# GQA attention: the second chunk's softmax reciprocal and its last multiplications come six steps later, behind the short chunk's

## The chip, the cores and the metric

One core of a Trainium2 chip runs the whole program. The metric is device time in microseconds (us). Before the change it is 3407.32 us, the median of three runs (3406.72 to 3411.54).

## What is computed

The reference is a block with sliding-window attention and an FFN, then two hybrid layers: one with grouped-query attention (GQA), one with MLA. The change lies in the GQA attention of the first hybrid layer alone:

```python
def gqa_attend(q, k, v):
    s = jnp.einsum('bqhgd,bkhd->bhgqk', q, k).astype(jnp.float32) * (GQA_HEAD_DIM ** -0.5)
    p = jax.nn.softmax(s, axis=-1).astype(v.dtype)
    return jnp.einsum('bhgqk,bkhd->bqhgd', p, v)
# 16 heads of 64; 1024 image queries see 256 + 1024 keys, 256 context queries see the 256 context keys;
# afterwards the output is multiplied by silu(g)
```

## The kernel before

**Chunks and steps.** Each head has three chunks of queries: chunk 0 and chunk 1 with 512 queries and ten tiles of 128 keys, and chunk 2, the short one, with 256 queries and two tiles of keys. One step is one tile of keys of one chunk, so a head has 22 steps: 0 to 9 are chunk 0, 10 to 19 chunk 1, 20 and 21 chunk 2. Heads follow each other without a break. Two heads make one turn of the loop, 44 steps. In this text a step number is that of its own head, and "a boundary" is the stretch in which one head ends while the next one runs its first steps.

**One step.** TensorE computes the transposed scores with two matrix products into one of two PSUM banks (L2371, L2372). ScalarE takes exp into `PF` (L2424) and rounds it into `PH` (L2430). GpSimd subtracts the two to get the low part `PL` (L2473); for steps 7, 9, 13 and 19 VectorE does this instead. TensorE then multiplies high and low parts with the values, three products into the output bank of the chunk (L2386 to L2388), three steps behind the scores. Chunks 0 and 1 have output banks of their own. Chunk 2 uses the bank `BC`, which also carries the transposed row maxima. The value tiles hold ones in their upper half, so the denominator stands in partitions 64 to 127 of the output bank.

**Row maxima.** The next chunk's maxima are prepared beside the steps: TensorE computes a tile of scores into `PMX` (L2341), VectorE reduces it (L2498), and when a chunk's tiles are done TensorE transposes them (L2352) and VectorE writes the row into `Q` (L2506). `PMX` holds one such tile, so TensorE can write the next one only when VectorE has reduced the one before. The plan by steps: tiles of the same head's chunk 1 at steps 0 (taken with the head before), 2 and 4, the short chunk's at 6, rows at 8 and 11, then the next head's chunk 0 at steps 10, 12, 14 and 16, its chunk 1's first at 18, a row at 20. In the last head steps 10 to 20 of this plan fall away.

**The end of a chunk.** ScalarE computes the reciprocal of the denominator with Ln and Exp into `RD` (L2440, L2442, function `rden`), between the exp and the rounding of a step. VectorE multiplies the output by it into `T` (L2517) and then `T` by the gate into `MIX` (L2522, function `final`). `RD` is one buffer, so a reciprocal waits for the multiplication into `T` before it. The counter `norm` counts these multiplications, and TensorE waits for it before it starts a chunk's output bank again.

**The order.** Each engine runs its own list, written out by hand. `lags` says how many steps behind its last step a chunk's end comes: on ScalarE 4, 4 and 5 steps for chunks 0, 1 and 2, on VectorE 8, 5 and 6. Within a step VectorE's list has first the maxima or row, then the low part of the step before where it is VectorE's, then the end of a chunk:

```python
if k and self.dve_lo(k - 1):
    self.low(dve, i, k - 1)
...
self.run(dve, step, lambda i, k: self.ended(final, i, k, self.lags), max(self.lags), ...)
```

So the head before has its chunk 1 reciprocal in step 1 and its end in step 2 of this head, and its chunk 2 reciprocal in step 4 and end in step 5.

SyncE issues the loads of keys, queries, values and the gate; the gate of a pair of heads is loaded once all ends of the pair before are done. After the last head, `MixSplit` splits `MIX` into a high and a low part (ScalarE L1889, VectorE L1893) for the output projection, the first three slices ahead of the last head's ends.

Of the kernel before, what the change touches and what calls it, by code (L numbers as in the profile page):

```python
# [104 lines left out]
def mixed_program(nc, A, out):  # L105

    ctx = ExitStack()
    with ctx:

        def sem(name):  # L110
            return ctx.enter_context(nc.semaphore(name))
# [4 lines left out]
        class Scope:  # L116


            def __init__(self):
                self.stack = ExitStack()  # L120
# [1981 lines left out]

        CR_PV2, CR_SC, CR_B, CR_E, CR_ROW2, CR_R, CR_N, CR_FIN2 = 4, 1, 2, 2, 1, 1, 4, 1

        def head_buffers(name, scope, q, layout, nq, side="left"):

# [8 lines left out]
        class Attention:  # L2117
# [9 lines left out]
            def __init__(self, name, scope, chunks, keys, scale, layout, mix, first, first_maxima):  # L2127
                self.name, self.chunks, self.keys, self.scale, self.mix = name, chunks, keys, scale, mix
                self.mla = layout == "mla"
                self.row = 96 if self.mla else 64  # L2130

                self.K, self.Q, self.V = zip(first, head_buffers(name, scope, 1, layout, chunks[-1][0] + chunks[-1][1]))
                self.G = scope.sb(f"{name}_gate", [P, chunks[-1][0] + chunks[-1][1]])
                self.PF = [scope.sb(f"{name}_pf{b}", [P, C]) for b in range(4)]
                self.PH = [scope.sb(f"{name}_ph{b}", [P, C], R32) for b in range(4)]
                self.PL = [scope.sb(f"{name}_pl{b}", [P, C], R32) for b in range(4)]
                self.M = first_maxima
                self.dim = 96 if self.mla else 64
                self.nq = chunks[-1][0] + chunks[-1][1]
                self.load_inc = 16 * (4 if self.mla else 6)  # L2140

                self.const_n = 32 + 4 + (32 + 2 if self.mla else 0)
                self.v_and_const = [sem(f"{name}_v_and_const{q}") for q in range(2)]
                self.RD = scope.sb(f"{name}_rd", [64, C])
                self.T = scope.sb(f"{name}_t", [P, C])
                self.loaded = [sem(f"{name}_loaded{q}") for q in range(2)]
                self.gate_loaded = sem(f"{name}_gate_loaded")
                (self.max, self.red, self.bcast, self.row_done, self.scores, self.exp, self.hi,
                 self.lo_pool, self.lo_dve, self.pv, self.rden, self.norm, self.fin) = [sem(f"{name}_{x}") for x in (
                     "max", "red", "bcast", "row", "scores", "exp", "hi", "lo_pool", "lo_dve", "pv",  # L2150
                     "rden", "norm", "fin")]
                self.S = [PB[0], PB[1]]
                self.BC = PB[2]
                self.FREE = self.BC if self.mla else PMX[:, 0:C]
                self.O = [PD[0], PD[1], self.BC]

                self.steps = [(q, c, t, x == 0, x == len(keys[c]) - 1) for q in range(2) for c in range(len(chunks))
                              for x, t in enumerate(keys[c])]
                self.SB = len(self.steps)
                self.NC = len(chunks)  # L2160

                if self.mla:
                    plan = [(2 * t, "max", (0, 1), t) for t in range(4)] + [(8, "bcast", (0, 1), 0)]
                    plan += [(10 + 2 * t, "max", (1, 0), t) for t in range(4)] + [(18, "bcast", (1, 0), 0)]
                    self.ahead = [(0, t) for t in range(4)]
                else:
                    plan = [(2 * t - 2, "max", (0, 1), t) for t in range(1, 4)] + [(6, "max", (0, 2), 0)]
                    plan += [(8, "bcast", (0, 1), 0), (11, "bcast", (0, 2), 0)]  # L2170
                    plan += [(10 + 2 * t, "max", (1, 0), t) for t in range(4)]
                    plan += [(18, "max", (1, 1), 0), (20, "bcast", (1, 0), 0)]
                    self.ahead = [(0, t) for t in range(4)] + [(1, 0)]
                self.plan = plan
                tiles = [p[2] for p in plan if p[1] == "max"]
                self.NT = len(tiles)
                self.last_tile = {group: n for n, group in enumerate(tiles)}
                self.fin_all = HEADS * self.NC + CR_FIN2
                self.norm_all = HEADS * self.NC + CR_N

                self.dve_lo = lambda k: k % (self.SB // 2) in ((3, 8, 13, 18) if self.mla else (7, 9, 13, 19))
                self.lags = (self.LAG + 4, self.LAG + 4, 0) if self.mla else (self.LAG + 5, self.LAG + 2, self.LAG + 3)
                self.n_dve = sum(1 for k in range(self.SB) if self.dve_lo(k))
                self.n_pool = self.SB - self.n_dve

# [134 lines left out]
            def pe_begin(self, pe):  # L2320
# [3 lines left out]
                SB, NC = self.SB, self.NC  # L2324
# [20 lines left out]
                def bcast(i, c, g, tile):  # L2345
                    n = self.chunks[c][1]
                    pe.wait_ge(self.red, i * (2 * self.NT) + (tile + CR_R + 1))

                    pe.wait_ge(self.row_done, i * (2 * NC) + (g + CR_ROW2))
                    if NC == 3:  # L2350
                        pe.wait_ge(self.norm, i * (2 * NC) + ((g - 1) // NC * NC + CR_N))
                    pe.matmul(self.BC[0:4, 0:n], self.M[g % 2][:, 0:4], ident[:, :].unsqueeze(1).to_broadcast([P, n // P, P]),  # L2352
                              start=True, stop=True).then_inc(self.bcast, 1)

# [20 lines left out]
                def values(i, k):  # L2375
                    q, c, t, first, last_ = self.steps[k]
                    n = self.chunks[c][1]
                    self.wait_lo(pe, i, k)
                    if first and c == 0:
                        pe.wait_ge(self.v_and_const[q], i * 32 + self.const_n)  # L2380
                    if first:

                        pe.wait_ge(self.norm, i * (2 * NC) + (q * NC + c - NC + CR_N + 1))
                    o = self.O[c][:, 0:n]
                    ph, pl = self.PH[k % 4][:, 0:n], self.PL[k % 4][:, 0:n]
                    pe.matmul(o, self.V[q][0][:, t, :], ph, start=first, stop=False)  # L2386
                    pe.matmul(o, self.V[q][1][:, t, :], ph, start=False, stop=False)  # L2387
                    pe.matmul(o, self.V[q][0][:, t, :], pl, start=False, stop=last_).then_inc(self.pv, 1)  # L2388
# [26 lines left out]
            def act_begin(self, act):  # L2415
                act.sem_inc(self.exp, CR_E)
                SB, NC = self.SB, self.NC
# [14 lines left out]
                def rden(i, k):  # L2432

                    q, c = self.steps[k][:2]
                    n = self.chunks[c][1]
                    x = q * NC + c
                    act.wait_ge(self.pv, i * SB + (k + CR_PV2 + 1))

                    act.wait_ge(self.norm, i * (2 * NC) + (x + CR_N))
                    act.activation(self.RD[:, 0:n], self.O[c][64:128, 0:n], ACT.Ln).then_inc(self.rden, 1)  # L2440
                    act.wait_ge(self.rden, i * (4 * NC) + (2 * x + 1))
                    act.activation(self.RD[:, 0:n], self.RD[:, 0:n], ACT.Exp, scale=-1.0).then_inc(self.rden, 1)  # L2442
# [1 line left out]
                def step(i, k, last, between):  # L2444
                    probs(i, k, between)

                lags, lag = (self.LAG + 1, self.LAG + 1, self.LAG + 2), self.LAG + (1 if self.mla else 2)

                def rest(split):
                    act.preload_act_table_set(LN_EXP)  # L2450
# [34 lines left out]
            def dve_begin(self, dve):  # L2485
                SB, NC, R = self.SB, self.NC, 2 * self.NT
# [23 lines left out]
                def final(i, k):  # L2510
                    q, c = self.steps[k][:2]
                    o, n = self.chunks[c]
                    x = q * NC + c
                    h = slice(64 * q, 64 * q + 64)
                    dve.wait_ge(self.rden, i * (4 * NC) + (2 * x + 2))
                    dve.wait_ge(self.fin, i * (2 * NC) + (x + CR_FIN2))
                    dve.tensor_tensor(self.T[h, 0:n], self.O[c][0:64, 0:n], self.RD[:, 0:n], ALU.mult)\  # L2517
                       .then_inc(self.norm, 1)
                    dve.wait_ge(self.norm, i * (2 * NC) + (x + CR_N + 1))
                    dve.wait_ge(self.gate_loaded, i * 16 + 16)  # L2520
                    m = self.mix[h, bass.ds(i, 1), o:o + n].rearrange("p o n -> p (o n)")
                    dve.tensor_tensor(m, self.T[h, 0:n], self.G[h, o:o + n], ALU.mult).then_inc(self.fin, 1)  # L2522
# [1160 lines left out]
```

## Time and profile before

| | |
|---|---|
| median of three runs | 3407.32 us |
| the profiled execution, its own time | 3410.39 us |
| its span | 3408.6 us |
| granted TensorE clock, mean | 0.993 |
| busy: TensorE, VectorE, ScalarE, GpSimd | 97%, 66%, 51%, 45% |
| GQA attention, from the first scores to the last values | 1770.5 to 2271.6 us |
| one turn of the loop (two heads) | 62.0 us |

The busy share of TensorE is no measure of its speed: a matrix product of 512 columns is shown as 390 ns long, while the next one starts 230 ns after it. So the starts are to be read, not the lengths. A wait of a few tenths hides in such a row.

### The profile page before, as it was taken

The page shows a single profiled execution, that of the slowest core. Times are in us where ns is not written, and L with a number is a line of the kernel's source. Part 1 is how long each engine was busy: PE and PEld are TensorE (multiplying, and loading weights), DVE is VectorE, ACT ScalarE, POOL GpSimd, SP SyncE. Part 2 cuts the span into 40 slices and gives each one's busy share as a digit, 9 for nine tenths or more (in the row PEclk, how much of TensorE's full clock was granted, in tenths as well). Part 3 has the DMA queues.
Part 4 walks back from the last instruction along what each step waited for, and adds up shares of the span by engine and source line. Part 5 has one row for each costly group of instructions (what it writes and reads, how often), then busy time and mean ns, then how long its engine had stood idle before and what let it go on. Part 6 is the DMA issues. An engine that isn't in the chain of part 4 may idle for free.

```text
span 3408.6 us, 48047 instructions
## 1 busy us (share of the span) xinstructions
PE 3292.7 (97%) x15029; PEld 2641.6 (77%) x15029; DVE 2259.8 (66%) x2664; ACT 1728.5 (51%) x2961; POOL 1522.3 (45%) x958
## 2 busy tenths in 40 slices
PE   9999999999999999999999999999998989999999
PEld 7778878778888888778877777778675668888877
DVE  7684878677576675648627777767558886666661
ACT  4343878332010111334328988871465658888880
POOL 2303444644444445520037777777220016666663
PEclk9999999999999999999999999999999999999999
DMA  3134231411212122123354354423255444332312
GB/s 111 50 117 132 56 89 51 154 53 55 91 48 94 49 75 73 39 85 111 121 138 89 81 108 100 88 65 116 102 193 157 130 128 120 69 80 62 80 38 80
DMA packets 196105, 313.57 MB, mean 92 GB/s; under 512 B 100944, under 2 KB 111696, under 8 KB 195984
## 3 DMA queue, kind: packets, MB, share of 16 engines
q1 hardware_dynamic: 195984, 312.01, 31.7%
q8 instruction: 70, 1.15, 0.1%
q14 instruction: 51, 0.42, 0.0%
HBM read 234.02 MB, written 77.92 MB: 92 GB/s over the span
## 4 chain that ended last, share of the span: by engine, by line
PE 64%; POOL 11%; issue 9%; DVE 9%; ACT 4%; DMA 1%; SPq 1%; POOLq 0%; DVEq 0%; ACTq 0%
PE PBX L285 11%; PE PBX L286 10%; PE PBX L287 10%; POOL gqa_pl L2473 9%; PE PMX L285 4%; PE PMX L286 4%; PE PMX L287 4%; PE PD L2386 2%; PE PMX L2341 2%; PE PD L2387 2%; PE PD L2388 2%; PE PBX L2368 2%; PE PBX L2367 2%; PE PBX L2369 2%; PE PD L1114 2%
## 5 line engine op out<-in xcount | busy, mean ns | idle before, releaser
L218 POOL TENSOR_TENSOR w_hi<-w_stage,zero 128x1024 fp32r<-128x1024 f32 (+2 forms) x114 | 222.3, 1950 | 1147.2 <-PE PBX L287 729.9
L2473 POOL TENSOR_TENSOR gqa_pl<-gqa_pf,gqa_ph 128x512 fp32r<-128x512 f32 (+1 forms) x288 | 371.1, 1309 | 141.2 <-ACT gqa_ph L2430 138.9
L2473 POOL TENSOR_TENSOR mla_pl<-mla_pf,mla_ph 128x512 fp32r<-128x512 f32 x256 | 341.4, 1339 | 194.6 <-ACT mla_ph L2430 189.6
L2498 DVE TENSOR_REDUCE mla_m<-PMX 128x1 fp32r<-128x1280 f32 x128 | 190.8, 1491 | 165.7 <-PE PMX L2341 165.6
L220 POOL TENSOR_TENSOR w_lo<-w_stage,w_hi 128x1024 fp32r<-128x1024 f32 (+2 forms) x114 | 289.2, 2537 | 9.0
L2498 DVE TENSOR_REDUCE gqa_m<-PMX 128x1 fp32r<-128x1280 f32 x144 | 201.5, 1399 | 133.1 <-PE PMX L2341 132.4
L2010 ACT ACTIVATE conv_in<-PBX 128x512 f32<-128x512 f32 x66 | 39.5, 599 | 478.8 <-PE PBX L287 474.8
L2424 ACT ACTIVATE mla_pf<-PBX 128x512 f32<-128x512 f32 x320 | 191.0, 597 | 81.8 <-PE PBX L2369 68.1
L2424 ACT ACTIVATE gqa_pf<-PBX 128x512 f32<-128x512 f32 (+1 forms) x352 | 200.0, 568 | 43.1 <-PE PBX L2372 40.4
L2430 ACT ACTIVATE gqa_ph<-gqa_pf 128x512 fp32r<-128x512 f32 (+1 forms) x352 | 215.0, 611 | 12.1
L285 PE MATMUL PBX<-ffn_hi,w_hi 128*128 128x512 f32 x528 | 206.8, 392 | 4.7 <-DVE ffn_lo L788 4.7
L2430 ACT ACTIVATE mla_ph<-mla_pf 128x512 fp32r<-128x512 f32 x320 | 201.9, 631 | 11.4
L287 PE MATMUL PBX<-ffn_hi,w_lo 128*128 128x512 f32 x528 | 205.5, 389 | 0.0
L286 PE MATMUL PBX<-ffn_lo,w_hi 128*128 128x512 f32 x528 | 205.5, 389 | 0.0
L2039 DVE SCALAR_TENSOR_TENSOR conv_out<-conv_in,VEC,conv_out 128x1024 f32<-128x1024 f32 x88 | 188.0, 2136 | 12.8 <-DVE conv_out L2035 0.6
L285 PE MATMUL PBX<-l_hi,w_hi 128*128 128x512 f32 (+1 forms) x400 | 157.8, 395 | 8.6 <-DVE l_lo L788 6.8
L484 DVE SCALAR_TENSOR_TENSOR PMX<-mod_w,cond_s 128x1024 f32<-128x1024 f32 x96 | 158.7, 1653 | 5.7 <-DVE PMX L484 0.8
L2035 DVE TENSOR_SCALAR conv_out<-conv_in,VEC 128x1024 f32<-128x1024 f32 x44 | 72.2, 1641 | 135.5 <-ACT conv_in L2010 134.7
L1723 POOL TENSOR_TENSOR swa_pl<-swa_pf,swa_ph 128x512 fp32r<-128x512 f32 x64 | 81.6, 1275 | 157.1 <-ACT swa_ph L1648 156.8
L287 PE MATMUL PBX<-l_hi,w_lo 128*128 128x512 f32 (+1 forms) x400 | 144.6, 361 | 0.0
L286 PE MATMUL PBX<-l_lo,w_hi 128*128 128x512 f32 (+1 forms) x400 | 144.4, 361 | 0.0
L285 PE MATMUL PBX<-h_hi,w_hi 128*128 128x512 f32 x336 | 139.0, 414 | 4.3 <-DVE h_lo L591 2.3
(534 smaller groups left out, 9882.1 us busy)
## 6 DMA issues: line engine op xcount, KB each, us to landing
mod_w<-in_w_mod SPq DMA_DIRECT2D x48, 512.0 KB, 3.5
w_stage<-in_w_up SPq DMA_DIRECT2D x44, 512.0 KB, 3.4
w_stage<-in_w_go SPq DMA_DIRECT2D x24, 512.0 KB, 3.7
gqa_k<-kh_d SPq DMA_DIRECT2D x32, 320.0 KB, 4.8
gqa_q<-qh_d SPq DMA_DIRECT2D x32, 320.0 KB, 7.0
w_stage<-in_w_down SPq DMA_DIRECT2D x24, 384.0 KB, 3.1
qh_d<-heads_qh SPq DMA_DIRECT2D x32, 256.0 KB, 2.1
ql_d<-heads_ql SPq DMA_DIRECT2D x32, 256.0 KB, 2.3
```

Of the source, the lines that this page charges most:

```text
L218: pool.tensor_tensor(w_hi[s][:, 0:st.cols], w_stage[s][:, 0:st.cols], z, ALU.add).then_inc(w_hi_done, 1)
L220: pool.tensor_tensor(w_lo[s][:, 0:st.cols], w_stage[s][:, 0:st.cols], w_hi[s][:, 0:st.cols].bitcast(F32), ALU.subtract).then_inc(w_split, 1)
L285: pe.matmul(ps, wh, xh, start=first, stop=False)
L286: pe.matmul(ps, wh, xl, start=False, stop=False)
L287: return pe.matmul(ps, wl, xh, start=False, stop=last)
L484: dve.scalar_tensor_tensor(out=PMX[:, C:3 * C], in0=bufs[s], scalar=1.0, in1=conds[j], op0=ALU.mult, op1=ALU.mult, accum_out=MOD[:, bass.d ...
L1723: pool.tensor_tensor(swa_PL[K % 4][:, :, 0:m], swa_PF[K % 2][:, :, 0:m], swa_PH[K % 4][:, :, 0:m].bitcast(F32), ALU.subtract).then_inc(a1[ ...
L2039: dve.scalar_tensor_tensor(out=y, in0=CU[s][:, j:j + S], scalar=w(j), in1=y, op0=ALU.mult, op1=ALU.add).then_inc(conv_step, 1)
L2424: act.activation(self.PF[k % 4][:, 0:n], self.S[k % 2][:, 0:n], ACT.Exp, scale=self.scale)\
L2430: act.activation(self.PH[k % 4][:, 0:n], self.PF[k % 4][:, 0:n], ACT.Copy).then_inc(self.hi, 1)
L2473: eng.tensor_tensor(self.PL[k % 4][:, 0:n], self.PF[k % 4][:, 0:n], self.PH[k % 4][:, 0:n].bitcast(F32), ALU.subtract).then_inc(self.lo_dv ...
L2498: dve.tensor_reduce(self.M[g % 2][:, t:t + n], PMX[:, 0:n * w].rearrange("p (n w) -> p n w", n=n), AX.X, ALU.max, negate=True).then_inc(se ...
```

## The change

On ScalarE chunk 1's reciprocal comes 10 steps behind the chunk's last step in place of 4. On VectorE its end comes 11 steps behind in place of 5. In the next head's count this is step 7 in place of 1, and step 8 in place of 2. The short chunk's stay in steps 4 and 5, so they now come first; `place` gives the new order for the counters, and `CR_N`, the credit of the counter `norm`, goes from 4 to 5, so that the waits mean the same buffers. MLA, which uses the same class, keeps its order.

```diff
-        CR_PV2, CR_SC, CR_B, CR_E, CR_ROW2, CR_R, CR_N, CR_FIN2 = 4, 1, 2, 2, 1, 1, 4, 1
+        CR_PV2, CR_SC, CR_B, CR_E, CR_ROW2, CR_R, CR_N, CR_FIN2 = 4, 1, 2, 2, 1, 1, 5, 1
...
-                self.lags = (self.LAG + 4, self.LAG + 4, 0) if self.mla else (self.LAG + 5, self.LAG + 2, self.LAG + 3)
+                self.place = (0, 1) if self.mla else (0, 2, 1)
+                self.lags = (self.LAG + 4, self.LAG + 4, 0) if self.mla else (self.LAG + 5, self.LAG + 8, self.LAG + 3)
...
                     if NC == 3:
-                        pe.wait_ge(self.norm, i * (2 * NC) + ((g - 1) // NC * NC + CR_N))
+                        pe.wait_ge(self.norm, i * (2 * NC) + ((g - 1) // NC * NC - 1 + CR_N))
...
-                        pe.wait_ge(self.norm, i * (2 * NC) + (q * NC + c - NC + CR_N + 1))
+                        pe.wait_ge(self.norm, i * (2 * NC) + (q * NC + self.place[c] - NC + CR_N + 1))
...
-                    x = q * NC + c
+                    x = q * NC + self.place[c]
                     act.wait_ge(self.pv, i * SB + (k + CR_PV2 + 1))
...
-                lags, lag = (self.LAG + 1, self.LAG + 1, self.LAG + 2), self.LAG + (1 if self.mla else 2)
+                lags = (self.LAG + 1, self.LAG + (1 if self.mla else 7), self.LAG + 2)
+                lag = max(lags[:NC])
...
-                    x = q * NC + c
+                    x = q * NC + self.place[c]
                     h = slice(64 * q, 64 * q + 64)
```

## Rows read from the trace of the kernel before

**Rows 1.** The page, the chain that ended last, by line.

```profile
PE PBX L285 11%; PE PBX L286 10%; PE PBX L287 10%; POOL gqa_pl L2473 9%; PE PMX L285 4%; PE PMX L286 4%; PE PMX L287 4%; PE PD L2386 2%; PE PMX L2341 2%; PE PD L2387 2%; PE PD L2388 2%; PE PBX L2368 2%; PE PBX L2367 2%; PE PBX L2369 2%; PE PD L1114 2%
```

**Rows 2.** Waits within the GQA attention: total us, times, longest.

```profile
PEld PD L2386 <- POOL gqa_pl L2473: 32.2, 81, 0.7
...
PE PMX L2341 <- DVE gqa_m L2498: 1.6, 2, 1.0
```

**Rows 3.** Timeline of TensorE, an odd head's steps 4 to 12: start, length, what.

```profile
1873.01 0.40 PE L2371 MATMUL PBX<-gqa_q,gqa_k 128*128 128x512 f32 x1
...
1873.64 0.50 PE L2386 MATMUL PD<-gqa_ph,gqa_v 128*128 128x512 f32 x1
...
1876.39 0.40 PE L2371 MATMUL PBX<-gqa_q,gqa_k 128*128 128x512 f32 x1
...
1877.54 0.39 PE L2371 MATMUL PBX<-gqa_q,gqa_k 128*128 128x512 f32 x1
...
1884.45 0.73 PE L2341 MATMUL PMX<-gqa_k,gqa_q 128*128 128x512 f32 x3
1885.02 0.40 PE L2371 MATMUL PBX<-gqa_q,gqa_k 128*128 128x512 f32 x1
```

**Rows 4.** Timeline of TensorE, the even head before it: its steps 4 and 12.

```profile
1841.96 0.39 PE L2371 MATMUL PBX<-gqa_q,gqa_k 128*128 128x512 f32 x1
...
1854.05 0.40 PE L2371 MATMUL PBX<-gqa_q,gqa_k 128*128 128x512 f32 x1
```

**Rows 5.** Timeline of ScalarE, the odd head's steps 1 to 12.

```profile
1869.82 0.59 ACT L2424 ACTIVATE gqa_pf<-PBX 128x512 f32<-128x512 f32 x1
...
1871.60 0.61 ACT L2430 ACTIVATE gqa_ph<-gqa_pf 128x512 fp32r<-128x512 f32 x1
...
1872.86 0.63 ACT L2430 ACTIVATE gqa_ph<-gqa_pf 128x512 fp32r<-128x512 f32 x1
...
1874.55 0.58 ACT L2424 ACTIVATE gqa_pf<-PBX 128x512 f32<-128x512 f32 x1
...
1875.89 0.62 ACT L2430 ACTIVATE gqa_ph<-gqa_pf 128x512 fp32r<-128x512 f32 x1
1876.53 0.60 ACT L2424 ACTIVATE gqa_pf<-PBX 128x512 f32<-128x512 f32 x1
1877.16 0.63 ACT L2430 ACTIVATE gqa_ph<-gqa_pf 128x512 fp32r<-128x512 f32 x1
...
1878.85 0.58 ACT L2424 ACTIVATE gqa_pf<-PBX 128x512 f32<-128x512 f32 x1
...
1885.76 0.60 ACT L2424 ACTIVATE gqa_pf<-PBX 128x512 f32<-128x512 f32 x1 [0.46 <-PE PBX L2372]
```

**Rows 6.** Timeline of VectorE, the odd head's steps 2 to 10.

```profile
1872.07 0.67 DVE L2517 TENSOR_TENSOR gqa_t<-PD,gqa_rd 64x512 f32<-64x512 f32 x1
1872.90 1.23 DVE L2522 TENSOR_TENSOR MIX<-gqa_t,gqa_gate 64x512 f32 x1
1874.06 1.47 DVE L2498 TENSOR_REDUCE gqa_m<-PMX 128x1 fp32r<-128x1280 f32 x1
...
1883.61 0.68 DVE L2473 TENSOR_TENSOR gqa_pl<-gqa_pf,gqa_ph 128x512 fp32r<-128x512 f32 x1
```

**Rows 7.** Timeline of GpSimd, the odd head's step 1.

```profile
1872.29 1.30 POOL L2473 TENSOR_TENSOR gqa_pl<-gqa_pf,gqa_ph 128x512 fp32r<-128x512 f32 x1 [1.01 <-ACT gqa_ph L2430]
```

**Rows 8.** Timelines of ScalarE and VectorE behind the last head.

```profile
2276.23 0.38 ACT L2440 ACTIVATE gqa_rd<-PBX 64x256 f32<-64x256 f32 x1 [1.53 <-DVE gqa_t L2517]
...
2275.46 0.68 DVE L2517 TENSOR_TENSOR gqa_t<-PD,gqa_rd 64x512 f32<-64x512 f32 x1
2276.18 0.69 DVE L2522 TENSOR_TENSOR MIX<-gqa_t,gqa_gate 64x512 f32<-64x512 f32 x1
2277.10 0.42 DVE L2517 TENSOR_TENSOR gqa_t<-PBX,gqa_rd 64x256 f32<-64x256 f32 x1 [0.23 <-ACT gqa_rd L2442]
...
2278.48 2.89 DVE L1893 TENSOR_TENSOR mix_l_lo<-MIX,mix_l_hi 128x1280 fp32r<-128x1280 f32 x2 [0.51 <-ACT mix_l_hi L1889]
```

## The prediction

> **What bounds the kernel now.** I read the page's chain first. Outside the projections it names GpSimd's low parts, L2473, with 9% of the span [rows 1], so the GQA attention isn't bound by TensorE alone. The waits within that stretch say how: the value products wait for low parts 81 times, 32.2 us in total; TensorE's maxima wait for VectorE's reduction only twice, 1.6 us [rows 2]. Then I read the timelines of one boundary step by step, because the waits don't tell which step is late and why.
>
> All sums below are counted from the start of the scores of step 4 to those of step 12. There the boundary's delays come to rest: at step 12 the exp starts 0.74 us behind its scores, which is the least it can be [rows 3, 5], and before step 4 TensorE loses nothing. The stretch takes 12.01 us in an odd head [rows 3] and 12.09 us in an even one [rows 4]. TensorE's own work in it: a step without maxima takes 1.15 us, five products at 0.23 [rows 3]; eight steps make 9.2. A tile of maxima takes 0.57 us [rows 3]; two whole ones, a short one of 512 columns (0.23) and two transposes (0.23 and 0.12) make 1.7. Together 10.9 us. So a boundary now costs TensorE 1.1 to 1.2 us of standing.
>
> The cause lies on ScalarE. A step there takes 1.16 us, two from exp(5) to exp(7) in 2.32 [rows 5], as much as TensorE's. The long reciprocal stretches the way from exp to rounding in step 1 to 1.78 us, against 0.63 in step 5 [rows 5]: 1.15 us. The short one, in step 4, makes it 1.34 [rows 5]: 0.7 us. With both, exp(4) starts 1.54 us behind its scores in place of 0.75 [rows 3, 5], the low parts are late, and TensorE waits for them.
>
> **The change, part by part.** Nothing is added or removed; two activations and two multiplications move. SyncE's list is untouched; its load of the gate waits for all ends of the pair before and so starts some three steps later, in step 8, while its first reader is in step 17. The second value chunk's first product needs the moved multiplication into `T` by step 13. `RD` and `BC` have their readers in the new order in time. These I cost at nothing; their cover is five steps or more.
>
> *Steps 1 and 2, what leaves.* Without the long reciprocal ScalarE keeps up: exp(4) starts 0.75 us behind the scores of step 4.
>
> *ScalarE, steps 4 to 7.* From the scores of step 4: exp(4) at 0.75; rounding (4) behind the short reciprocal at +1.34 = 2.09; exp(5) +0.64 = 2.73; exp(7) +2.32 = 5.05 [rows 5]. Now the long reciprocal stands here: rounding (7) at +1.78 = 6.83, done 0.61 later, 7.44. Rounding (8) follows +1.26 behind rounding (7), as (2) behind (1) [rows 5]: 8.09.
>
> *What is queued behind it.* Low part 7 is VectorE's own. In the old place the delayed rounding (1) fed GpSimd. Behind low part 7 in VectorE's list stand now the two multiplications of the chunk's end, and behind them the reduction of the first maxima tile of step 10, and for that reduction TensorE waits before it can write the tile of step 12. GpSimd starts a low part 0.69 us behind the start of its rounding [rows 5, 7], 0.08 behind its end; I take the same 0.08 for VectorE. Low part 7 then starts at 7.52 and takes 0.68 [rows 6]: 8.20. The multiplication into `T` starts then, and the one into `MIX` 0.83 later [rows 6]: 9.03.
>
> *The multiplication into MIX.* Alone it takes 0.69 us [rows 8]. In the boundary it took 1.23: it started at 1872.90 while GpSimd worked on a low part until 1873.59, and it ended at 1874.13, 0.54 behind that [rows 6, 7]. So it stands still until GpSimd's instruction is over. In the new place GpSimd takes up low part 8 at 8.09 + 0.69 = 8.78, 0.25 us before 9.03, and holds until 10.08 (1.30 long). The multiplication ends at 10.62. The Trainium skill, page "SBUF — State Buffer", section "Who interferes with whom", says the same of any VectorE instruction with two SBUF inputs against a GpSimd one that reads SBUF: whoever comes first keeps the shared ports, the other blocks. By that rule, as by the rows, the sum has 1.59 us here; by the plain length it would have 0.69 and end in the second rival below.
>
> *The reduction and TensorE.* The reduction follows its multiplication at once and takes 1.47 [rows 6]: 12.09. TensorE takes up released work 0.05 us after (low part done at 1873.59, product at 1873.64 [rows 3, 7]): 12.14. The maxima tile takes 0.57 [rows 3], so the scores of step 12 start at 12.71. TensorE itself would be there at 10.9; whatever it loses in steps 7 and 11 for low parts 4 and 8 lies within these 1.8 us.
>
> So the boundary gives back its 1.1 to 1.2 us of waiting for low parts and pays 1.8 us of waiting for a reduction: +0.62 us in an even head (12.71 against 12.09), +0.70 in an odd one. Seven even heads (2 to 14) and seven odd ones (1 to 13) have it: 7 x 0.62 + 7 x 0.70 = +9.2 us.
>
> *The last head* has no maxima from step 10 on. It is bound by ScalarE from end to end, so it loses what ScalarE idles: the long reciprocal's 1.15 no longer fills its wait of 1.54 - 0.75 = 0.79 us before exp(4): +0.4 us.
>
> *Behind the last head* the order of the two ends turns round. Now the long multiplication into `T` starts at 2275.46 and frees `RD` at 2276.14, the short reciprocal starts at 2276.23 and the short multiplication at 2277.10 [rows 8]. New: the short multiplication (0.42) frees `RD` at 2275.88; the long reciprocal starts at 2275.97; the way from there to its multiplication is the short one's 0.87 plus 0.2 for each of its two activations, 2277.25; that takes 0.68 (2277.93), the one into `MIX` 0.69 more behind 0.15 (2278.77). The next split, now at 2278.48, is put off by 0.3 us, and TensorE waits for it.
>
> **Sum.** 9.2 + 0.4 + 0.3 = +9.9 us. The rows come from one execution with a time of 3410.39 us, 3.1 above the median of the runs, and a span of 3408.6; the difference carries over, so I add it to the median: 3407.3 + 9.9 = 3417.2 us. By the side of the unknown costs: if rounding (7) and low part 7 are up to 0.1 us quicker or slower on each of 14 boundaries, the sum moves by 1.4; if TensorE's restart costs 0.3 more, by 4. Its own range is 3414 to 3422.
>
> **Rivals.**
>
> *The multiplication comes before GpSimd.* Decided by one thing: 9.03 against 8.78. If VectorE is 0.25 us sooner, or low part 8 that much later, the multiplication ends at 9.72, the reduction at 11.19 and step 12 starts at 11.81: 0.28 and 0.20 us less than now, 14 boundaries -3.4, with the ends -2.7, 3404.6 us. For it: the margin is small. Against it: each term between them is an instruction behind another on the same engine, and these repeat to some hundredths.
>
> *ScalarE's relief is all that counts (faster).* TensorE runs free through the boundary if the reduction is done when it comes for the tile of step 12, at about 10.2. Then the stretch takes 10.9, -1.1 to -1.2 us each, 14 boundaries -16.5, with the ends -15.8: 3391.5 us. For it: the wait for low parts is the only one of weight now [rows 2]. Against it: the chain above passes 10.2 with the reduction not yet begun. It decides if the reduction starts before 8.7, that is if VectorE reaches it before the chunk's end.
>
> *The delay runs on (slower still).* Behind the late reduction VectorE has low part 9 (0.68) [rows 6], then the row of step 11, then the reduction of the tile of step 12. GpSimd has low part 10 from about 11.1 to 12.4, low part 9 is asked for at 12.1 and gets its turn in between. If low part 11 slips in ahead of it, the next reduction is 1.1 us later, and TensorE's slack there is 0.1: 14 x 1.1 = +15.4 more, 3432.6 us. For it: the margin. Against it: VectorE asks first.
>
> **How the numbers follow.** I give the forecast 0.60, the multiplication first 0.17, the free run 0.13, the delay that runs on 0.10. What this kernel's measurement can tell from no change is about 0.2%, 6.8 us. The first and the last case are slower by more, 0.70, of which I take 0.02 away for a boundary cost of under 0.4 us; the second is within, which makes 0.18 with some of that; faster 0.14. The range from 3403 to 3426 us holds the forecast, the second case and part of the last; it leaves out the free run and the full run-on, some 2 in 10.
>
> **What would show it.** In the profile after: no standing of the value products in steps 4 and 5 of more than 0.3 us; the long reciprocal behind exp(7) and rounding (7) 1.78 us after it; the multiplication into `MIX` about 1.6 us long, its end 0.5 behind the end of a GpSimd low part; the reduction of step 10's tile right behind it; and a new wait of TensorE's maxima L2341 for the reduction L2498, 1.2 to 1.8 us, 14 times. A turn of the loop should take 63.3 us in place of 62.0. The prediction is wrong if that wait is missing or under 0.5 us, or if the multiplication takes 0.7.

## The result: 0.37% slower

The changed kernel takes 3422.75 us (median of 8 runs, 3418.43 to 3424.90), the kernel before beside it 3407.67. The ratio is 1.0037 with a 95% interval of 1.0028 to 1.0046, so it is slower by 9.5 to 15.7 us; forecast were 9.9. The profiled execution took 3423.56 us with a span of 3421.8, 13.2 more than before.

**The new wait.** The waits within the GQA attention after the change: total us, times, longest.

```profile
PEld PMX L2342 <- DVE gqa_m L2500: 23.2, 16, 1.5
PEld PD L2387 <- POOL gqa_pl L2475: 21.8, 64, 0.9
...
PE PMX L2342 <- DVE gqa_m L2500: 16.2, 16, 1.1
```

Against [rows 2]: the value products' wait for low parts has fallen from 32.2 to 21.8 us, and TensorE's maxima now wait 16 times for VectorE's reduction, 2 of them as before and 14 new. (PEld is TensorE's weight load, PE its product; they stand in the same wait, so the two totals are not to be added.)

**One boundary.** The timeline of ScalarE in an odd head, steps 4 to 8. The scores of its step 4 start at 1874.68.

```profile
1875.42 0.60 ACT L2425 ACTIVATE gqa_pf<-PBX 128x512 f32<-128x512 f32 x1
...
1876.78 0.61 ACT L2431 ACTIVATE gqa_ph<-gqa_pf 128x512 fp32r<-128x512 f32 x1
1877.42 0.60 ACT L2425 ACTIVATE gqa_pf<-PBX 128x512 f32<-128x512 f32 x1
...
1879.74 0.58 ACT L2425 ACTIVATE gqa_pf<-PBX 128x512 f32<-128x512 f32 x1
1880.34 0.60 ACT L2441 ACTIVATE gqa_rd<-PD 64x512 f32<-64x512 f32 x1
1880.97 0.63 ACT L2443 ACTIVATE gqa_rd<-gqa_rd 64x512 f32<-64x512 f32 x1
1881.51 0.61 ACT L2431 ACTIVATE gqa_ph<-gqa_pf 128x512 fp32r<-128x512 f32 x1
```

Exp(4) follows its scores by 0.74 us, where it was 1.54 [rows 3, 5]: ScalarE is relieved at the head of the boundary. Exp(7) starts at 1879.74, rounding (7) at 1881.51, 1.77 later: the long reciprocal stands there now.

The timeline of VectorE behind it, and of GpSimd beside it:

```profile
1882.16 0.69 DVE L2475 TENSOR_TENSOR gqa_pl<-gqa_pf,gqa_ph 128x512 fp32r<-128x512 f32 x1 [1.42 <-ACT gqa_ph L2431]
1882.77 0.68 DVE L2519 TENSOR_TENSOR gqa_t<-PD,gqa_rd 64x512 f32<-64x512 f32 x1
1883.58 1.74 DVE L2524 TENSOR_TENSOR MIX<-gqa_t,gqa_gate 64x512 f32 x1
1885.25 1.47 DVE L2500 TENSOR_REDUCE gqa_m<-PMX 128x1 fp32r<-128x1280 f32 x1
1886.65 0.94 DVE L2475 TENSOR_TENSOR gqa_pl<-gqa_pf,gqa_ph 128x512 fp32r<-128x512 f32 x1
```

```profile
1883.49 1.29 POOL L2475 TENSOR_TENSOR gqa_pl<-gqa_pf,gqa_ph 128x512 fp32r<-128x512 f32 x1 [2.04 <-ACT gqa_ph L2431]
```

Low part 7, the multiplication into `T`, the one into `MIX`, the reduction: each follows the one before. The one into `MIX` starts 0.09 us after GpSimd has begun low part 8, and ends 0.54 after GpSimd's end (1884.78). It is 1.74 us long; alone it takes 0.69 [rows 8].

And TensorE, steps 11 and 12:

```profile
1885.40 0.40 PE L2389 MATMUL PD<-gqa_pl,gqa_v 128*128 128x512 f32 x1
1886.78 0.86 PE L2342 MATMUL PMX<-gqa_k,gqa_q 128*128 128x512 f32 x3 [0.98 <-DVE gqa_m L2500]
1887.47 0.40 PE L2372 MATMUL PBX<-gqa_q,gqa_k 128*128 128x512 f32 x1
```

It would have gone on at 1885.63 and starts at 1886.78, when the reduction is over: 1.15 us of standing. From the scores of step 4 to those of step 12 it is 12.79 us here and 12.93 in the even heads, against 12.01 and 12.09 [rows 3, 4]. From step 12 to the next head's step 0 nothing changed (13.86 and 13.87). A turn of the loop takes 63.6 us in place of 62.0.

### The profile page after: what moved, and what is told of

The parts are those of the page before. It is cut to its first block, busy times and chain, and to the rows that moved or that the text cites. A ratio compares the mean times of both kernels' runs of the same rounds, so it can differ in the third digit from the quotient of the medians.

```text
span 3421.8 us, 48053 instructions
## 1 busy us (share of the span) xinstructions
PE 3293.7 (96%) x15029; PEld 2642.9 (77%) x15029; DVE 2262.7 (66%) x2664; ACT 1728.7 (51%) x2961; POOL 1521.3 (44%) x958
## 3 DMA queue, kind: packets, MB, share of 16 engines
q8 instruction: 70, 1.15, 0.1%
## 4 chain that ended last, share of the span: by engine, by line
PE 65%; POOL 11%; issue 9%; DVE 9%; ACT 4%; DMA 1%; SPq 0%; POOLq 0%; DVEq 0%; ACTq 0%
PE PBX L285 10%; PE PBX L286 10%; PE PBX L287 10%; POOL gqa_pl L2475 8%; PE PMX L285 4%; PE PMX L286 4%; PE PMX L287 4%; PE PMX L2342 2%; PE PD L2387 2%; PE PD L2388 2%; PE PD L2389 2%; PE PBX L2369 2%; PE PBX L2368 2%; PE PBX L2370 2%; PE PD L1114 2%
```

## The experiments

In this table the stretch is read from the starts of the first score product of steps 4 and 12, odd head and even head; heads 1 to 14 agree within 0.1 us, but for head 14 of e_dve (12.66). Each ratio compares a kernel with runs of the kernel before made beside it, whose medians lie between 3407.41 and 3408.71 us.

| kernel | steps 4 to 12, us | turn, us | median, us | ratio to the kernel before |
|---|---|---|---|---|
| before | 12.01, 12.09 | 62.0 | | |
| changed | 12.79, 12.93 | 63.6 | 3422.75 | 1.0037 [1.0028, 1.0046] |
| e_nogate | 11.56, 11.56 | 61.0 | 3401.21 | 0.9979 [0.9970, 0.9988] |
| e_port | 11.81, 12.03 | 62.4 | 3412.95 | 1.0016 [1.0006, 1.0025] |
| e_low6 | 11.97, 11.97 | 61.9 | 3407.46 | 0.9998 [0.9988, 1.0007] |
| e_late | 11.55, 11.54 | 61.0 | 3400.62 | 0.9984 [0.9975, 0.9993] |
| e_dve | 12.30, 12.43 | 63.3 | 3414.74 | 1.0022 [1.0011, 1.0033] |
| e_end10 | 11.55, 11.55 | 62.9 | 3414.09 | 1.0016 [1.0007, 1.0026] |
| e_norec | 11.75, 11.85 | 61.5 | 3405.53 | 0.9994 [0.9985, 1.0004] |
| e_rec9 | 11.23, 11.32 | 60.6 | 3399.37 | 0.9976 [0.9967, 0.9985] |
| e_b_nogate | 12.00, 12.08 | 62.0 | 3408.69 | 1.0002 [0.9992, 1.0011] |
| e_b_both | 11.21, 11.36 | 60.5 | 3396.19 | 0.9966 [0.9953, 0.9978] |

Theory A is that of the prediction: the reduction of step 10's tile is late because the chunk's end stands ahead of it on VectorE, and that end is long because it starts behind a delayed low part and waits for GpSimd. Theory B blames the late reciprocal on ScalarE by itself. In the diffs below `...` stands for lines that are not shown.

### e_nogate: no gate multiplication

```diff
...
+                    if c == 1 and not self.mla:
+                        dve.tensor_tensor(m, self.O[c][0:64, 0:n], self.RD[:, 0:n], ALU.mult).then_inc(self.norm, 1)
+                        dve.wait_ge(self.norm, i * (2 * NC) + (x + CR_N + 1))
+                        dve.wait_ge(self.gate_loaded, i * 16 + 16)
+                        dve.memset(self.T[h, 0:8], 0.0).then_inc(self.fin, 1)
+                        return
...
```

> The changed kernel, but for chunk 1 the multiplication by the gate is left out: the first multiplication writes into MIX itself, and a memset of 8 columns keeps the count. Theory A (the reduction of step 10's tile is late because it stands behind the chunk's end on VectorE, above all behind the gate multiplication that waits for GpSimd's low part 8): the reduction starts 8.9 us after the scores of step 4 in place of 10.6, and steps 4 to 12 take about 11.2 us in place of 12.8 and 12.9; 14 boundaries give -23 us against the changed kernel, about 3400 us, some 8 us faster than the kernel before. Theory B (the late reciprocal on ScalarE delays exps and low parts, and the reduction's wait only stands where TensorE would have waited anyway): no more than -3 us, 3420 us.

Measured 11.56 us for the stretch and 3401.21 us. Its waits:

```profile
PEld PD L2387 <- POOL gqa_pl L2475: 22.5, 67, 0.7
...
PE PMX L2342 <- DVE gqa_m L2500: 1.6, 2, 1.0
```

The reduction's wait is back to the 2 times of [rows 2]. Theory A holds, B falls as the account of the loss: the reciprocal stands where the change put it, and the boundary costs 1.2 to 1.4 us less than in the changed kernel. The stretch came out 0.36 longer than forecast; what is left of waiting is for low parts (22.5 us in all, 67 times).

### e_port: the same two multiplications without two SBUF inputs

```diff
...
+                        dve.wait_ge(self.gate_loaded, i * 16 + 16)
+                        dve.tensor_tensor(self.T[h, 0:n], self.O[c][0:64, 0:n], self.G[h, o:o + n], ALU.mult)
+                        dve.tensor_tensor(m, self.O[c][0:64, 0:n], self.RD[:, 0:n], ALU.mult).then_inc(self.norm, 1)
+                        dve.wait_ge(self.norm, i * (2 * NC) + (x + CR_N + 1))
+                        dve.memset(self.T[h, 0:8], 0.0).then_inc(self.fin, 1)
+                        return
...
```

> The changed kernel, but the two multiplications of chunk 1's end read the PSUM bank and one buffer each (T from the output and the gate, MIX from the output and the reciprocal, so the gate is missing in MIX), and a memset of 8 columns keeps the count. VectorE does two multiplications of the same size as before, none with two SBUF inputs. Theory A1 (the wait for GpSimd is the larger part of the cost): the pair takes 1.4 us in place of 2.6, steps 4 to 12 take about 11.8 us in place of 12.8 and 12.9, -15 us against the changed kernel, about 3408 us. Theory A2 (it is VectorE's own work in that place that counts, whatever its inputs): the pair still takes 2.6 us, 3422 us.

The timeline of VectorE in the same boundary as above:

```profile
1882.49 0.67 DVE L2522 TENSOR_TENSOR gqa_t<-PD,gqa_gate 64x512 f32<-64x512 f32 x1
1883.09 0.67 DVE L2523 TENSOR_TENSOR MIX<-PD,gqa_rd 64x512 f32 x1
1883.82 0.07 DVE L2525 MEMSET gqa_t<- 64x8 f32 x1
1883.96 1.49 DVE L2500 TENSOR_REDUCE gqa_m<-PMX 128x1 fp32r<-128x1280 f32 x1
```

GpSimd's low part 8 runs from 1883.21 to 1884.51 here too, across the second multiplication and the start of the reduction, and neither is longer for it. The pair takes 1.3 us in place of 2.6. The odd stretch is 1.0 us shorter than in the changed kernel, as A1 said, the even one 0.9. A2 falls. The even heads 2 to 12 are also 0.6 us longer from step 12 on (14.49 against 13.87), so the whole came out at 3413, not 3408. VectorE's timeline in the next head, an even one, shows where:

```profile
1916.37 1.75 DVE L2475 TENSOR_TENSOR gqa_pl<-gqa_pf,gqa_ph 128x512 fp32r<-128x512 f32 x1
1918.15 0.41 DVE L2508 TENSOR_TENSOR gqa_q<-PBX,ident_f 4x256 fp32r<-4x256 f32 x1
1918.60 1.49 DVE L2500 TENSOR_REDUCE gqa_m<-PMX 128x1 fp32r<-128x1280 f32 x1
```

Low part 9, two SBUF inputs as well, is 1.75 us long in place of 0.68: GpSimd began low part 10 at 1916.29, 0.08 us earlier. The Trainium skill, page "SBUF — State Buffer", section "Who interferes with whom", has the same: VectorE with two SBUF inputs contends with a GpSimd instruction that reads SBUF, with at most one it doesn't. TensorE then stands for low part 9 itself, at its value product of step 12, as the waits of e_port show:

```profile
PEld PD L2387 <- DVE gqa_pl L2475: 4.8, 6, 0.8
```

The product starts 0.51 us late and the next one 0.11 later still, which are the 0.6. The reduction of step 12 follows late as well, but TensorE doesn't stand for it at step 14. So this is not the third rival of the prediction (low part 11 ahead of low part 9, and a stand for the next reduction), but a neighbour of it that the prediction doesn't have, set off by a shift of some tenths.

### e_low6: VectorE takes low part 6, GpSimd low part 7

```diff
-                self.dve_lo = lambda k: k % (self.SB // 2) in ((3, 8, 13, 18) if self.mla else (7, 9, 13, 19))
+                self.dve_lo = lambda k: k % (self.SB // 2) in ((3, 8, 13, 18) if self.mla else (6, 9, 13, 19))
```

> The changed kernel, with VectorE taking low part 6 and GpSimd low part 7 (dve_lo 6, 9, 13, 19). The chunk's end no longer stands behind the low part whose rounding the long reciprocal delays. Theory A: the first multiplication starts with the reciprocal, 6.95 us after the scores of step 4 in place of 8.09; the gate multiplication then waits for GpSimd's low part 7 and ends at about 9.4 in place of 10.65; steps 4 to 12 take 11.6 us, -1.2 to -1.3 each, -17 us against the changed kernel, about 3405 us. Theory B (the late reciprocal itself): unchanged within 3 us, 3420 to 3425.

The loss is gone (0.9998), and the maxima wait only twice, with the reciprocal still in step 7: theory B falls here too. But the stretch is 11.97, not 11.6. The timeline of GpSimd shows why:

```profile
1881.32 1.29 POOL L2475 TENSOR_TENSOR gqa_pl<-gqa_pf,gqa_ph 128x512 fp32r<-128x512 f32 x1 [2.02 <-ACT gqa_ph L2431]
```

```profile
1882.61 1.70 POOL L2475 TENSOR_TENSOR gqa_pl<-gqa_pf,gqa_ph 128x512 fp32r<-128x512 f32 x1
```

These are low parts 7 and 8. Low part 7 now comes from the slower engine right behind the delayed rounding, low part 8 waits for it and is 0.41 us longer, since the gate multiplication got in between. TensorE's product of step 8 starts at 1884.36, 0.05 after its low part. I had followed VectorE's list and not the low parts themselves.

### e_late: the gate multiplication goes to step 13

```diff
                        .then_inc(self.norm, 1)
+                    if c != 1 or self.mla:
+                        gated(i, k)
...
+                    GATED = self.LAG + 13
+                    def finish(i, k):
+                        self.ended(final, i, k, self.lags)
+                        if not self.mla:
+                            x = k - GATED
+                            if x < self.SB and self.steps[x][4] and self.steps[x][1] == 1:
+                                gated(i, x)
...
```

Here `gated` holds the gate multiplication as it was.

> The changed kernel with chunk 1's end divided: the multiplication into T stays in step 8, the gate multiplication goes to step 13, behind the reduction of step 12. Theory A: the reduction of step 10's tile starts 8.8 us after the scores of step 4, TensorE doesn't wait for it, steps 4 to 12 take 11.1 us; in step 13 the gate multiplication has some 1.4 us before the next reduction, so that this one is up to 0.3 us late, within TensorE's slack. -24 us against the changed kernel, about 3399 us, 0.25% faster than the kernel before. Rival: the wait for GpSimd only moves to step 13 or 14 and delays the reduction there (a stand of 0.5 to 1 us at step 14 or 16): 3407 to 3415 us.

```profile
1878.36 0.68 DVE L2519 TENSOR_TENSOR gqa_t<-PD,gqa_rd 64x512 f32<-64x512 f32 x1
1878.96 1.47 DVE L2500 TENSOR_REDUCE gqa_m<-PMX 128x1 fp32r<-128x1280 f32 x1
...
1882.01 1.49 DVE L2500 TENSOR_REDUCE gqa_m<-PMX 128x1 fp32r<-128x1280 f32 x1 [0.54 <-PE PMX L2342]
1883.42 1.05 DVE L2532 TENSOR_TENSOR MIX<-gqa_t,gqa_gate 64x512 f32 x1
1884.88 1.49 DVE L2500 TENSOR_REDUCE gqa_m<-PMX 128x1 fp32r<-128x1280 f32 x1 [0.41 <-PE PMX L2342]
```

On VectorE's timeline the reduction follows the first multiplication, and in step 13 the gate multiplication has room: the next reduction again waits for TensorE (0.41), not TensorE for it. With all work done, this is 0.16% faster than the kernel before (0.9984, 0.9975 to 0.9993). The rival falls. The stretch is 11.55 and not 11.1: by the starts of its products TensorE loses 0.27 us at low parts 4 to 6, behind the short reciprocal, and 0.30 at low part 8, behind the long one.

### e_dve: VectorE's half of the change alone

```diff
+                self.RD1 = self.RD if self.mla else scope.sb(f"{name}_rd1", [64, C])
...
-                lags = (self.LAG + 1, self.LAG + (1 if self.mla else 7), self.LAG + 2)
-                lag = max(lags[:NC])
+                lags = (self.LAG + 1, self.LAG + 1, self.LAG + 2)
+                lag = self.LAG + (1 if self.mla else 2)
...
```

> Only VectorE's half of the change: chunk 1's reciprocal stays in step 1 on ScalarE, with a buffer RD1 of its own, and its two multiplications come in step 8, behind the short chunk's. Theory A (two costs: the place on ScalarE gives or takes some tenths, the place on VectorE makes the reduction late): low part 7 is done 7.8 us after the scores of step 4, the gate multiplication waits for GpSimd's low part 8 until 9.6 and ends at 10.2, steps 4 to 12 take 12.3 us, +0.2 to +0.3 against the kernel before on 14 boundaries, +4 us, 3411 to 3412 us. Rival (the whole loss comes from VectorE's half): 12.8 us and 3420 us.

The stretch took 12.30 and 12.43 us: 0.3 of the loss of 0.8 in it comes with VectorE's half alone, as theory A has it, and the rival falls. What was not forecast is a further 0.3 to 0.4 us behind step 12 (14.2 us against 13.9 to the next head's step 0): low part 9 met GpSimd's, took 1.48 us, and TensorE stood for it. The median is 3414.74 us, not 3411 to 3412. The other half of the change is no gain in this stretch but a further cost. The timelines of GpSimd and VectorE, from scores of step 4 at 1872.54, show where it comes from:

```profile
1880.86 1.29 POOL L2477 TENSOR_TENSOR gqa_pl<-gqa_pf,gqa_ph 128x512 fp32r<-128x512 f32 x1 [0.76 <-ACT gqa_ph L2432]
```

```profile
1881.39 1.31 DVE L2526 TENSOR_TENSOR MIX<-gqa_t,gqa_gate 64x512 f32 x1
```

Low part 8 starts 8.32 us after the scores of step 4, and the gate multiplication, which waits for it, ends at 10.16. With the reciprocal in step 7 they are at 8.81 and 10.64, since the rounding of step 8 is late. Low part 7 has no share in it: it is done at 8.12 here and at 8.17 there.

### e_end10: the whole end in step 10

```diff
-                self.lags = (self.LAG + 4, self.LAG + 4, 0) if self.mla else (self.LAG + 5, self.LAG + 8, self.LAG + 3)
+                self.lags = (self.LAG + 4, self.LAG + 4, 0) if self.mla else (self.LAG + 5, self.LAG + 10, self.LAG + 3)
```

> The changed kernel with chunk 1's whole end two steps later, in step 10 behind the reduction and low part 9 (lag 13 in place of 11). Theory A: the reduction of step 10's tile is free, steps 4 to 12 take about 11.5 us; but the end now stands before the row of step 11 and the reduction of step 12's tile, waits for GpSimd's low part 10, and that reduction ends about 1.1 us after TensorE comes for step 14's tile. So steps 12 to the next head's 0 take about 14.9 us in place of 13.9: a gain of 0.2 to 0.4 us a boundary against the changed kernel, 3417 to 3420 us. Rival (any place behind the reduction of step 10 is free): 13.9 us there, 3402 us.

Measured 11.55 and, from step 12 on, 14.80 us, both as theory A has them. The stand has moved to step 14; the timeline of TensorE:

```profile
1889.61 0.85 PE L2342 MATMUL PMX<-gqa_k,gqa_q 128*128 128x512 f32 x3 [0.97 <-DVE gqa_m L2500]
```

So an end, 2.4 us with its wait for GpSimd, costs ahead of the reduction of step 10 and between that one and step 12's just as well; TensorE asks for a reduction every second step. The rival falls. Of places further on no run has the whole end. The median is 3 us below the forecast of 3417 to 3420.

### e_norec, e_b_nogate, e_b_both: what the boundary waited for before

Three kernels on the kernel before, to see whether the relief that the change aims at is there.

```diff
+                    if c == 1 and not self.mla:
+                        n = 8
                     act.activation(self.RD[:, 0:n], self.O[c][64:128, 0:n], ACT.Ln).then_inc(self.rden, 1)
```

> The kernel before with chunk 1's reciprocal computed for 8 columns of 512 (the others keep older values). Theory A (before, the boundary waits because ScalarE has the long reciprocal and the short one there): what is left of the two activations is their fixed part, about 0.4 of 1.15 us; steps 4 to 12 take about 11.3 us in place of 12.0 and 12.1, -11 us, 3396 us. Rival (the boundary waits because VectorE's gate multiplications hold up GpSimd's low parts 2 and 4, 1.72 us long in place of 1.30): 12.0 us and 3406 us.

> The kernel before, with chunk 1's gate multiplication left out (the multiplication by the reciprocal writes into MIX itself, a memset of 8 columns keeps the count); the reciprocal stays whole. If ScalarE's reciprocals alone set the boundary of the kernel before, steps 4 to 12 stay at 12.0 us. If VectorE's gate multiplication has a share by way of low part 2 (1.72 us long in place of 1.30) and the reduction of step 4, they take about 11.6 us, -3 us in all.

> The kernel before, with chunk 1's reciprocal computed for 8 columns of 512 and its gate multiplication left out as well. If two covers lie over each other (the reciprocal on ScalarE, and the gate multiplication that makes the reduction of step 4's tile late), taking both gives more than the sum of the two alone: steps 4 to 12 take 11.0 to 11.2 us, -7 us in all. If the rest of the wait has another cause, they stay at 11.7.

Less reciprocal shortens the stretch by 0.25 us, not by 0.75; leaving out the gate multiplication alone changes nothing; both together give 0.7 to 0.8. So something else takes up the relief when ScalarE alone is relieved. In e_norec the timelines of VectorE, GpSimd and TensorE show it, in an odd head whose scores of step 4 start at 1871.54:

```profile
1871.42 1.68 DVE L2524 TENSOR_TENSOR MIX<-gqa_t,gqa_gate 64x512 f32 x1
1873.03 1.47 DVE L2500 TENSOR_REDUCE gqa_m<-PMX 128x1 fp32r<-128x1280 f32 x1
```

```profile
1871.26 1.30 POOL L2475 TENSOR_TENSOR gqa_pl<-gqa_pf,gqa_ph 128x512 fp32r<-128x512 f32 x1
```

```profile
1874.56 0.51 PE L2341 MATMUL PMX<-gqa_k,gqa_q 128*128 128x256 f32 x2 [0.57 <-DVE gqa_m L2500]
```

It is the same mechanism as after the change, in step 6: a gate multiplication, lengthened by GpSimd, ahead of a reduction. The kernel before did not have this wait. There the reduction ended at 1875.53 [rows 6], and TensorE came for the tile of step 6 only 0.63 us later:

```profile
1876.16 0.40 PE L2341 MATMUL PMX<-gqa_k,gqa_q 128*128 128x256 f32 x2
```

Counted from the scores of step 4, the reduction ends at 2.52 us before and at 2.96 in e_norec. With ScalarE relieved GpSimd is one low part further on: the gate multiplication meets low part 2 at its start and takes 1.68 us, where it met low part 1 in its middle and took 1.23. In e_b_both, without the multiplication, TensorE comes for this tile at 2.29; in e_norec it starts it at 3.02. Of these 0.73 us the relief itself made 0.44. The median of e_norec (0.9994) is too near the kernel before to show the 0.25 us a boundary; its trace shows them.

### e_rec9: a version from what was found

```diff
-                self.lags = (self.LAG + 4, self.LAG + 4, 0) if self.mla else (self.LAG + 5, self.LAG + 8, self.LAG + 3)
+                self.lags = (self.LAG + 4, self.LAG + 4, 0) if self.mla else (self.LAG + 5, self.LAG + 10, self.LAG + 3)
...
-                lags = (self.LAG + 1, self.LAG + (1 if self.mla else 7), self.LAG + 2)
+                lags = (self.LAG + 1, self.LAG + (1 if self.mla else 9), self.LAG + 2)
```

with the divided end of e_late.

> A version put together from what was found: reciprocal in step 9 (whose low part VectorE takes), multiplication into T in step 10 behind the reduction and low part 9, gate multiplication in step 13. Theory A: low part 8 is no longer held up, TensorE keeps only the waits of steps 5 and 7; steps 4 to 12 take about 11.1 us in place of 11.55 with the gate multiplication in step 13 alone; the reduction of step 12 is 0.5 us late, within TensorE's slack of 0.6. -6 us against that version, 3394 us. Rival (the multiplication into T ahead of the row and of step 12's reduction costs what end 10 costs): a stand of 0.5 to 1 us at step 14, 3401 to 3408 us.

```profile
1881.97 0.68 DVE L2519 TENSOR_TENSOR gqa_t<-PD,gqa_rd 64x512 f32<-64x512 f32 x1
1882.68 0.42 DVE L2508 TENSOR_TENSOR gqa_q<-PBX,ident_f 4x256 fp32r<-4x256 f32 x1
1883.12 1.49 DVE L2500 TENSOR_REDUCE gqa_m<-PMX 128x1 fp32r<-128x1280 f32 x1
1884.53 1.22 DVE L2532 TENSOR_TENSOR MIX<-gqa_t,gqa_gate 64x512 f32 x1
```

The multiplication into `T`, 0.68 long, fits ahead of the row and of step 12's reduction, where the whole end did not: TensorE has no stand at step 14, and the rival falls. The stretch is 11.23 and 11.32 us, a turn 60.6. It takes 3399.37 us where 3394 were forecast, 0.24% less than the kernel before (0.9967 to 0.9985), the lowest median of those that do all the work. Against e_late it is 0.4 us a turn quicker by the traces; the medians of the two are 1.2 us apart and their intervals overlap, which shows no difference by itself. The stand for low part 8 is gone (53 waits for low parts in place of e_late's 67): 0.2 to 0.3 us a head are what the reciprocal in step 7 costs by itself. In the changed kernel they lie within the wait for the reduction.

## Why the prediction was right, and where it was off

Direction and mechanism came out as forecast, and nearly every step of the chain with its size. Us after the scores of step 4, odd head and even head:

| step of the working | predicted | measured |
|---|---|---|
| exp(4) | 0.75 | 0.74, 0.75 |
| rounding (7) | 6.83 | 6.83, 6.83 |
| low part 7 done | 8.20 | 8.17, 8.17 |
| multiplication into `MIX` starts | 9.03 | 8.90, 9.03 |
| GpSimd starts low part 8 | 8.78 | 8.81, 8.82 |
| multiplication into `MIX` ends | 10.62 | 10.64, 10.66 |
| reduction ends | 12.09 | 12.04, 12.18 |
| scores of step 12 | 12.71 | 12.79, 12.93 |

The new wait was forecast as 1.2 to 1.8 us; it is 1.15 by the starts of the products (1885.63 to 1886.78), since TensorE loses time at low parts 4 and 8 first, as the working allowed for. Also, the prediction says that the multiplication's plain length would lead to its second rival; its sums (9.72, 11.81) are those of the first.

**The largest error** is in the last term: from the maxima tile to the scores I took 0.57 us, the price in a running TensorE [rows 3]. Where TensorE has stood it is 0.69 (1886.78 to 1887.47): the product after the first follows at 0.34 us and not at 0.23. The trace of the kernel before had this, at a value product that had waited for its low part (1873.64, the next at 1873.98). It is 0.12 us on 14 boundaries, 1.7 us. The reduction in the even heads ended 0.09 later than summed, 0.6 us more. The 14 boundaries gave 7 x 0.78 + 7 x 0.84 = 11.3 us in place of 9.2.

**The first rival** (the multiplication ahead of GpSimd) was nearer than I had it: in the odd heads the margin was 0.09 us, since a VectorE instruction may start up to 0.08 before the end of the one ahead of it. It happened in none of the 14 boundaries: the multiplication takes 1.62 to 1.74 us in all of them. e_port, whose multiplication doesn't wait, has 11.81 in the odd heads, as the rival said, and 12.03 in the even ones. **The free run** would have needed the reduction 1.9 us sooner; e_nogate and e_late are near it, at 11.55 and not 10.9, because low parts 4 to 6 and 8 hold TensorE (0.27 and 0.30 us). **The run-on** did not come: steps 12 to 0 are unchanged in the changed kernel. What came in the even heads of e_port and in e_dve is a neighbour of it: low part 9 met GpSimd's low part 10, took 1.75 and 1.48 us, and TensorE stood for low part 9 itself.

**The picture of the kernel before** was incomplete. I put the boundary's wait down to ScalarE. That it sets the wait there e_b_nogate shows (12.00 and 12.08 without the gate multiplication). But relieving ScalarE alone gives 0.25 us and not 0.75 (e_norec), because the gate multiplication, which then meets GpSimd's next low part, delays a reduction that TensorE waits for; it is the mechanism that I had put down as the new one. The change moved both at once, so this did not bear on its sum.

**The ends.** The last head cost 0.3 us by its last value product (11.7 us late, with 11.3 from the boundaries and 0.1 from the first head), forecast 0.4; behind it 0.33, forecast 0.3: 12.07 in all against 9.9. The profiled execution is another 1.1 us longer in code that the change doesn't touch, behind 2420 us. In e_late the code behind the attention ran 2.4 us shorter than before. The first head differs too. TensorE stands there 2.0 to 2.8 us for a load of values, and behind it the traces of before and of e_late have, from 1788 to 1791 us (busy times of PE, PEld, DVE, ACT and POOL with the number of instructions, granted clock, DMA share, GB/s):

```profile
1788.00:1791.00 3.00, 3.00 (x9) 2.17 (x8) 2.16 (x3) 1.70 (x3) 1.33 (x1) 0.50 0.02 5
```

```profile
1788.00:1791.00 3.00, 3.00 (x15) 2.38 (x14) 2.51 (x4) 2.46 (x4) 1.59 (x2) 1.00 0.02 5
```

At a granted clock of 0.50 (1.2 in place of 2.4 GHz) TensorE has 9 products there in place of 15, and steps 4 to 12 of the first head take 16.21 us in place of 14.45. The changed kernel's trace has the slow form too (16.29), and so have e_low6, e_norec and e_rec9; the other traces have the quick one (14.4 to 14.7), e_b_nogate among them, which has the kernel before's order. So it adds nothing to the 13.2 us between the two spans, but some 2 us between two traces can be this. The median's 15.1 us has its interval from 9.5 to 15.7, and the 12.07 lie in it; what the other 3 are no run here shows. The median lies in the range given (3403 to 3426), but 0.75 us above the narrower one of the sum (3414 to 3422).

## What to carry to other kernels

When an instruction moves past others on an in-order queue, ask what stands behind it at the new place, and who waits for that: here the moved work found VectorE idle and was still in the way, because TensorE asks for a reduction every second step and a 2.6 us pair doesn't fit between two. Cost a moved two-input VectorE operation with its wait for GpSimd, and look whether it can be divided: the short part that frees the bank early, the long part where there is room. And before you count on the relief of one engine, redo the times of the others with it: here the relief brought a gate multiplication onto the next low part and was mostly lost.

## What the runs showed of the hardware

A VectorE multiplication of two SBUF inputs, 64x512, takes 0.69 us alone [rows 8]. Started while a GpSimd subtraction from SBUF runs, it ends 0.54 us after that one's end, so it takes up to 1.74; the GpSimd instruction that follows is in its turn longer, by 0.41 us in e_low6 (1.70 against 1.29) and by 0.45 in e_norec (1.74). With one of the inputs in PSUM it stays at 0.67 beside the same GpSimd instruction (e_port). After a stand TensorE's second product starts 0.34 us after the first, in place of 0.23, at a granted clock of 1.00 both times. Behind the stand of 2.0 to 2.8 us in the first head the granted clock was 0.50 in five of the twelve traces and 1.00 in seven. VectorE's instructions start up to 0.08 us before the shown end of the one ahead where it waits for nothing, and some 0.15 after it where one reads the other's result.
